# The conditioning weights of a hybrid decoder step: tiles of two channel tiles by 512 columns against one by 1024, and passes of 128 against 256 columns

## What is computed

```python
mod = (jax.nn.silu(c) @ ada_w[i] + ada_b[i]).reshape(c.shape[0], N_MOD, D_MODEL)
hn = modulate(x, norm_g[i, 0], mod[:, 0], mod[:, 1])
...
x = x + mod[:, 2][:, None, :] * out
```

## Time and profile before

| | before |
|---|---|
| median of 3 executions | 1377.57 us (1377.35 to 1378.26) |
| span of the profiled execution | 1376.5 us |
| mean granted TensorE clock | 0.989 |
| PE busy | 1328.3 us, 96% |
| DVE, POOL, ACT busy | 52%, 38%, 26% |
| DMA | 169.34 MB, mean 123 GB/s |

### The profile page before, as it was taken

The page is one execution under the profiler, slowest core; times in us unless marked ns, Lnnn a source line. Parts: engine busy times, 40 slices in busy tenths (PEclk is TensorE's granted clock), DMA queues, the critical chain, the costliest instruction groups (busy, mean ns, idle before and its releaser), DMA issues.

```text
span 1376.5 us, 26372 instructions
## 1 busy us (share of the span) xinstructions
PE 1328.3 (96%) x11593; PEld 1291.6 (94%) x11593; DVE 720.0 (52%) x1124; ACT 362.4 (26%) x560; POOL 524.6 (38%) x248
## 2 busy tenths in 40 slices
PE   5899999999999999999999999999989999999997
PEld 4799889999899999999999999999989999999996
DVE  2714445677931541441548819759871551641774
ACT  3532443222421221221223333122321221211311
POOL 2433424433333333434334344434334444343440
PEclk9899999999999999999999999999999999999999
DMA  9675213654455446445442233223133323323321
GB/s 330 201 195 145 66 53 115 219 167 143 138 160 178 151 127 190 153 145 170 152 141 83 59 105 89 86 75 105 49 93 92 90 81 91 91 80 91 93 62 65
DMA packets 239804, 169.34 MB, mean 123 GB/s; under 512 B 5691, under 2 KB 211775, under 8 KB 239562
## 3 DMA queue, kind: packets, MB, share of 16 engines
q1 hardware_dynamic: 215946, 121.33, 29.9%
q10 hardware_dynamic: 23584, 46.27, 10.5%
q0 software_dynamic: 160, 0.07, 0.0%
HBM read 160.70 MB, written 6.94 MB: 122 GB/s over the span
## 4 chain that ended last, share of the span: by engine, by line
PE 82%; DVE 10%; issue 3%; ACT 2%; DMA 1%; POOL 1%; ACTq 0%; SPq 0%; POOLq 0%; DVEq 0%
PE G L1527 55%; PE G L1553 19%; PE B L1623 3%; DVE acc L997 1%; DVE hb L1120 1%; DVE small_s L1467 1%; DVE yc L1466 1%; DMA xin<-in_x_sample 1%; PE B L1813 1%; PE B L1513 1%; ACT wh L457 1%; DVE Xl L1134 1%; PE B L1815 1%; PE B L1885 1%; DVE sqb L959 1%
## 5 line engine op out<-in xcount | busy, mean ns | idle before, releaser
L818 POOL TENSOR_TENSOR wl<-raw,wh 128x1024 fp32r<-128x1024 f32 x192 | 483.9, 2523 | 684.9 <-ACT wh L457 681.9
L457 ACT ACTIVATE wh<-raw 128x1024 fp32r<-128x1024 f32 x192 | 202.8, 1057 | 475.7 <-PE G L1527 190.7
L1527 PE MATMUL G<-Xh,wh 128*128 128x272 f32 x960 | 205.5, 296 | 5.0 <-ACT stage L464 4.0
L1527 PE MATMUL G<-Xl,wh 128*128 128x272 f32 x960 | 199.4, 289 | 0.0
L1527 PE MATMUL G<-Xh,wl 128*128 128x272 f32 x960 | 198.3, 288 | 0.0
L1527 PE MATMUL G<-Hh,wh 128*128 128x272 f32 x864 | 180.2, 290 | 0.0
L1527 PE MATMUL G<-Hl,wh 128*128 128x272 f32 x864 | 178.6, 288 | 0.0
L1527 PE MATMUL G<-Hh,wl 128*128 128x272 f32 x864 | 177.5, 287 | 0.0
L1527 PEld LDWEIGHTS G<-Xh,wh 128*128 128x128 f32 x960 | 150.6, 190 | 11.0 <-issue 8.7
L976 DVE TENSOR_TENSOR small_s<-G,modT 128x32 f32<-128x32 f32 x80 | 15.2, 190 | 264.9 <-PE G L1527 202.9
L1527 PEld LDWEIGHTS G<-Xl,wh 128*128 128x128 f32 x960 | 152.0, 190 | 0.0
(11 more groups left out here) (324 smaller groups left out, 2021.9 us busy)
## 6 DMA issues: line engine op xcount, KB each, us to landing
aring<-in_ada_w ACTq DMA_DIRECT2D x78, 512.0 KB, 4.8
raw<-in_mlp_w_up SPq DMA_DIRECT2D x64, 512.0 KB, 4.0
raw<-in_mlp_w_down SPq DMA_DIRECT2D x64, 512.0 KB, 3.6
raw<-in_mlstm_w_in SPq DMA_DIRECT2D x24, 512.0 KB, 4.1
raw<-in_conv_w_in SPq DMA_DIRECT2D x24, 512.0 KB, 3.8
early<-in_ada_w SPq DMA_DIRECT2D x16, 512.0 KB, 12.4
raw<-in_mlstm_w_out SPq DMA_DIRECT2D x8, 512.0 KB, 5.3
raw<-in_conv_w_out SPq DMA_DIRECT2D x8, 512.0 KB, 3.6
```

Of the source, the lines that this page charges most:

```text
L457: nc.scalar.activation(wh[:, t % SLOTS], raw[:, t % RAWS], ACT.Copy).then_inc(s_hi, 1)
L818: nc.gpsimd.tensor_tensor(wl[:, t % SLOTS], raw[:, t % RAWS], wh[:, t % SLOTS].bitcast(F32), ALU.subtract).then_inc(s_lo, 1)
L1527: last = mm(G[:, 2 * (g % 2) + hf, 0:HALF], w[:, s, k, :], x[:, k, hf * HALF:(hf + 1) * HALF], start=st, stop=en)
```

## The change

The tile of `ada_w` becomes one channel tile (128 rows) by 1024 columns: one run of 4 KB into each partition. Tile `a` of a block is then channel tile `a % 8`, and each group has one matmul of 256 columns for it. The 512 KB of a tile, the number of tiles and pairs, their places in the order of work, the semaphores and the result's layout in `ada_out` stay. The constant `QW` (512) goes.

```diff
-GROUPS, GW, QW = 4, 32, 512
+GROUPS, GW = 4, 32
...
-        early1 = sb("early1", [P, 8, 2, QW], at=at_X)
+        early1 = sb("early1", [P, 8, D], at=at_X)
...
-        aring = sb("aring", [P, ADAS, 2, QW])
+        aring = sb("aring", [P, ADAS, D])
...
-        early0 = sb("early0", [P, 8, 2, QW], at=at_w)
+        early0 = sb("early0", [P, 8, D], at=at_w)
...
-            n, quad, k = ADA_ORDER[a // KT], a // 4 % 2, 2 * (a % 4)
-            src = ins["ada_w"][n // NMOD].rearrange("(k p) n -> p k n", p=P)
-            c = n % NMOD * D + QW * quad
-            queue.dma_start(ada_tile(a), src[:, k:k + 2, c:c + QW])\
+            n, k = ADA_ORDER[a // KT], a % KT
+            c = n % NMOD * D
+            queue.dma_start(ada_tile(a), ins["ada_w"][n // NMOD][k * P:(k + 1) * P, c:c + D])\
                 .then_inc(s_ada[a % ADAS] if a >= ADA_RING else s_early[a], 16)
...
-                n, quad = k // 4, k // 2 % 2
+                n = k // 4
...
-                    for r in range(2):
-                        kk = 2 * (a % 4) + r
-                        for g in range(GROUPS):
-                            columns = ada_tile(a)[:, r, :].rearrange("p (t g c) -> p g t c", t=GROUPS, g=GROUPS)[:, g]
-                            last = mm(ada_out[GW * g:GW * (g + 1), P * quad:P * (quad + 1)], cpad[:, kk, :], columns,
-                                      start=(kk == 0), stop=(kk == KT - 1), tile_position=(0, GW * g))
+                    for g in range(GROUPS):
+                        columns = ada_tile(a).rearrange("p (t g c) -> p g t c", t=KT, g=GROUPS)[:, g]
+                        last = mm(ada_out[GW * g:GW * (g + 1), :], cpad[:, a % KT, :], columns,
+                                  start=(a % KT == 0), stop=(a % KT == KT - 1), tile_position=(0, GW * g))
                     last.then_inc(s_au, 1)
```

## The result

The changed kernel takes 1379.39 us (median of 20 executions, 1377.61 to 1385.54) against 1377.87 us before (20 executions, 1374.95 to 1380.83). The ratio is 1.0018, 95% interval 1.0011 to 1.0025: it is slower, where 1376.0 us was forecast, 1.5 us less, within 1373.6 to 1378.8. The ratio stands for 2.5 us; the means (1380.24 and 1378.06 us) are 2.2 apart and the medians 1.5, so the size is known to about 1 us. The profiled execution of it has a span of 1379.5 us and a mean granted clock of 0.987.

What follows compares the result with a forecast made beforehand. PE's work was taken as the bound, with the input's landing at the start. Savings of 1.4 us (pairs), 0.04 (pairs 4 to 7) and 0.1 (`xin`) gave 1.5 us off 1377.57: 1376.0 us, range 1373.6 to 1378.8.

Steps and rivals of the forecast that it cites:

- The round: Four matmul groups running together on PE, eight such per pair before; said to be bound by columns, which the change keeps.
- `xin`: Input at the start, queued behind two `ada_w` tiles; forecast to land 0.1 us sooner through 4 KB runs.
- pairs 4 to 7: Conditioning pairs on the chain at the start; forecast 0.04 us less, taking 5.3 us with no DMA wait.
- The pair, 0.035 us: Saving claimed for each of 40 conditioning pairs in the main stream behind 60 us, 1.4 us in all.
- The first round of a pair: At each pair's start on PE, an uncovered weight load was to be covered by longer columns: 0.025 us less.
- point (3): In the pair's matmuls on PE: half the instruction issue goes, said to cost nothing as four start together.
- A: Faster: the pair's time that isn't columns belongs to instructions; half gone gives 3.5 us, 1374.1, all gives 1370.7; 12%.
- B: In the pairs, each weight load waits for its matmul; fewer loads give 19.4 us less, 1358; 2%.
- C: Slower: early tiles stream worse in 4 KB runs, pairs 4 to 7 end 9.3 us later, 1387; 6%.
- E: The compiler splits the longer pass, or the drain grows with it, so nothing is gained: 1377.5; 10%.
- D: A DVE and POOL collision while POOL forms `wl`: one PE stall more or less, 6 us, 1382 or 1370; 4%.

Runs made afterwards that it cites:

- early_new: Kernel before with the new tile shape only for the sixteen early tiles (blocks 0 and 1): 1377.81 us, ratio 0.9999.
- one_block: Kernel before with the new shape for one block alone, the second early one (eight tiles): 1382.08 us, ratio 1.0026.
- one_block_old: Changed kernel with the old shape for the second early block alone, 88 of 96 tiles in the new shape: 1378.15 us, ratio 0.9997.
- after_spread: Changed kernel with the fourth pair of each block in layer 0's MLP behind the eighth tile instead of the seventh: 1377.58 us, ratio 0.9987.
- after_pad: Changed kernel plus 128 instructions of already satisfied semaphore waits in TensorE's stream: 1380.09 us, ratio 1.0018.
- spread_one_old: Changed kernel with the second early block in the old shape and layer 0's fourth MLP pairs behind the eighth tile: 1376.58 us, ratio 0.9989.
- spread_pad_after: Changed kernel with layer 0's fourth MLP pairs behind the eighth tile and 128 padding wait instructions in TensorE's stream: 1377.62 us, ratio 0.9996.
- ring_gap: Kernel before with only the 80 ring tiles in the new shape, a 16-byte SBUF gap cutting runs to 2 KB: 1380.29 us, ratio 1.0009.
- after_again: The changed kernel run again without edit, against the kernel before: 1379.87 us, ratio 1.0017.
- late_new: Kernel before with the new shape only for blocks 4 to 11 (64 tiles, fetched behind 230 us): 1378.33 us, ratio 1.0002.
- before_pad: Kernel before plus 128 instructions of already satisfied semaphore waits in TensorE's stream: 1385.46 us, ratio 1.0047.

## Why the prediction was wrong

**What held.** The round is bound by its columns: 0.379 us is 0.273 + 0.106, and the pair's columns didn't get cheaper or dearer. `xin` landed 0.38 us sooner, of which 0.1 was forecast, and pairs 4 to 7 took 5.23 us without waiting for a tile. With 4 KB runs the DMA engines moved 408 GB/s in 16 to 30 us against 387. That gain was in the sum with the right sign and nothing came of it that the ratios can show: early_new, which has all of it, is at 0.9999.

**The pair, 0.035 us.** This term was mis-sized: 0.010 us, its lower bound. The first round of a pair still costs 0.025 us over the step (starts 0, 0.240, 0.456 and 0.672 us). I had taken it for a weight load that 0.107 us of columns can't cover; under 0.213 us of columns it is the same, so it isn't that. 40 pairs give 0.4 us and not 1.4.

**The step that failed.** It is point (3), "half the issue of instructions, which cost nothing". The sum asked what the missing instructions save at their own place and gave nothing to what they move. They are 98 KB of TensorE's stream, and the fetches of 16 KB behind the missing ones come at another time. One then fell on ACT's DMA issue at 138 us, in the heads, where ACT, DVE and PE wait for each other in turn. Rivals A, B, C and E looked at the new tiles or products, and D at another collision. In eight profiles with the fetch there (seven kernels and a repeat) the two issues took 1.59 to 1.89 us and tile 11 13.8 us or more; in nine profiles of the others 1.10 and 13.31 us. one_block makes the loss with a twelfth of the change, and one_block_old takes it away with eleven twelfths in place. In these two the fetch is all that moves in that stretch; every later fetch of TensorE moves with it.

The issues for ring tiles say the same of the whole kernel. In the seventeen profiles ACT made 1326 of them. At 74 the issue took 1.0 us or more, and each of these had a fetch under way; 110 more overlapped a fetch and took less.

A rule of the Trainium skill bears on this. Runtime: NRT & Kernel Launch, Instruction fetch mechanics, says that each engine's instructions are refilled in blocks of 16 KiB and that crossing a boundary is "mostly hidden". The size agrees with the rows. For TensorE it is hidden here too, with tiles 44 to 59 at 106.81 or 106.82 us in four profiles of the two kernels; for the DMA issue of another engine it was not, by 0.5 to 0.8 us.

**How 0.6 us becomes 2.5.** The pairs give -0.4 us, tile 11 +0.6. Tiles 16 and 17 give +0.4, and the chain names the cause: a tile of `raw` that lands late.

```profile
215.71 5.81 DMA raw<-in_mlstm_w_in
```

What ACT waited for there, before and then after:

```profile
ACT wh L457 <- DMA raw<-in_mlstm_w_in: 0.3, 1, 0.3
```

```profile
ACT wh L456 <- DMA raw<-in_mlstm_w_in: 1.8, 1, 1.8
```

In the eight profiles with the slow issue this tile landed 5.2 to 6.1 us after its issue, and a fetch fell between the two; in the nine others it took 4.2 to 4.5 us, without a fetch between. ACT waited 1.1 to 2.1 us for it against 0.2 to 0.5. Tiles 16 and 17 took 19.87 to 20.43 us in seven of the eight, in place of 19.64 to 19.67; after_spread took 19.66, and after_pad, of the others, 21.04 with a fall of the clock there. So this loss goes with the place of the fetches too; it was not switched apart from the one at 138 us.

The rest is the clock. Between tiles 11 and 15 it was at 0.50 for 4.7 us on average over the eight profiles with the slow issue (0 to 6.8) and for 1.5 over the nine others (0 to 3.4); half of 3.2 us is 1.6 us of work. The mean granted clock of all executions gives the same: 0.9878 in 32 of the changed kernel and 0.9890 in 35 of the kernel before, and the difference of 0.0012 over 1378 us is 1.6 us. The sum is -0.4 + 0.6 + 0.4 + 1.6 = 2.2 us, against 2.2 between the means and 2.5 by the ratio.

That a longer stall makes the fall likelier is an inference, not a thing that was switched by itself. The granted clocks put a limit to it. By the same reckoning spread_one_old, after_pad and spread_pad_after, whose issue is fast, lost 2.3, 1.7 and 2.2 us more than the kernel before beside them, and ring_gap, whose issue is slow, 0.2 (give or take 0.8 to 2.0 us). So the clock also falls for reasons that these runs don't name. Rival D had the price of such a fall and the wrong trigger.

**Late ring tiles.** PE's waits for ring tiles behind 60 us, 0.4 to 1.0 us in all, stand in after_again, ring_gap, late_new, after_spread, before_pad and one_block, and in neither profile of before. The ring holds one pair, and where two pairs are a tile apart a pair lands 0.5 to 1.0 us ahead of its use. In before_pad and one_block, which have the old shape in the ring, the issue of the late tile itself met a fetch (1.18 and 1.69 us in place of 0.49). In the other four it took its usual time, and all four have the new products in the ring, ring_gap with runs of 2 KB. What delays them stays open; late_new's interval bounds it at 0.14%.

## What to carry to other kernels

When a change takes instructions out of a long stream or adds them, count their bytes and see in the trace where the instruction fetches of that engine move, above all against DMA issues that stand on the chain. Test a result of 0.2% by moving the stream alone, best with a part of the change in a place that is done (the padding had a cost of its own), before believing that the new code is slow. And look where PE waits anyway, as at a change of unit: a piece of independent work put there was worth more (0.9982) than any reshaping of that work.

## What the runs showed of the hardware

- A DMA issue by ACT of 0.61 us took 1.10 to 1.40 us when an instruction fetch of 16 KB, 0.9 to 1.4 us long, was under way, in all eight profiles where they met. Overlap alone isn't enough: of 184 issues for ring tiles that met a fetch, 74 took 1.0 us or more; of 1142 that met none, none did.
- A 512 KB tile by SP near 215 us landed after 5.2 to 6.1 us with one such fetch in between (eight profiles) and after 4.2 to 4.5 us without (nine).
- With 64 instructions that only wait on a semaphore with its value reached put between pairs 3 and 4, PE stood idle for 5.6 to 6.3 us there in the three padded kernels, with no wait that the profile shows; in the others it stood 4.5 us, for DVE.
- At the same stall of 1.6 us near 175 us, the clock fell to 0.50 for 0 and 3.4 us in two executions of the kernel before, and for 6.8 and 3.4 in two of the changed one; two profiles of the kernel before differ by 1.0 to 1.6 us in a stretch for that reason.
- Tiles in runs of 4 KB keep the DMA engines no longer in all (3.18 us of each engine for a pair between 230 and 710 us, 3.21 before), with a median of 159 ns for a packet in place of 84; those over 500 ns are 4.5% of the packets in place of 1.2%.
